# Two transformer blocks in float32 on one core: wait counts in the delta rule, PSUM banks and split order in the feed-forward blocks, and one pool unit's evacuation

## The reference

```python
merged = sigmoid(g_a) * pool_mixer(u_pool, ...) + sigmoid(g_b) * conformer_conv(u_glu, ...)
# delta rule, per head (8 heads) and chunk of 64 tokens (8 chunks)
Lmat = where(strict, (kb @ k.T) * decay, 0)          # Gram matrices
sol = triangular_solve(eye + Lmat, rhs)
v_new = val - kcd @ state
o = qd @ state + a_c @ v_new
state = state * gl + kd.T @ v_new
# feed-forward block (twice), FFN_DIM = 2816
u = causal_dwconv(h @ w_up, conv_w) + conv_b         # 2 x 2816 columns
gate, up = split(u, 2)
h = h + (silu(gate) * up) @ w_down
```

## Time and profile before

| | |
|---|---|
| median of 3 runs | 1963.59 us (1961.83 to 1964.22) |
| profiled execution, its own time | 1957.58 us |
| span of that execution | 1955.6 us |
| mean granted TensorE clock | 0.99 of full speed |

### The profile page before, as it was taken

How to read it: one execution, slowest core, us unless ns; L and a number is a source line. 1 busy time by engine, 2 the same in 40 slices (tenths; PEclk the granted TensorE clock), 3 DMA queues, 4 the chain that set the end, 5 groups by cost and what they waited for, 6 DMA issues and landing times.

```text
span 1955.6 us, 29679 instructions
## 1 busy us (share of the span) xinstructions
PE 1887.9 (97%) x10628; PEld 1525.9 (78%) x10628; DVE 1203.9 (62%) x1851; ACT 787.6 (40%) x1495; POOL 274.3 (14%) x213
## 2 busy tenths in 40 slices
PE   7999999999998899999999999999999999999997
PEld 6888878888887677777778878888776788788886
DVE  5997554333334777677645746747688657467474
ACT  4234343223233555455433423424546534234242
POOL 2532232101022100001011101101100111001012
PEclk9999999999998999999999999999999999999998
DMA  5222323232322111111112332222321122322321
GB/s 193 97 97 97 129 77 102 92 101 93 99 95 76 49 63 58 60 61 49 50 55 90 104 108 86 97 97 97 108 65 44 57 84 99 114 88 91 102 89 72
DMA packets 46945, 170.47 MB, mean 87 GB/s; under 512 B 5344, under 2 KB 5504, under 8 KB 46720
## 3 DMA queue, kind: packets, MB, share of 16 engines
q1 hardware_dynamic: 45648, 165.12, 25.3%
q10 hardware_dynamic: 1200, 3.95, 0.6%
HBM read 166.94 MB, written 2.11 MB: 86 GB/s over the span
## 4 chain that ended last, share of the span: by engine, by line
PE 79%; DVE 10%; ACT 5%; issue 4%; POOL 1%; DVEq 0%; DMA 0%; ACTq 0%; POOLq 0%; SPq 0%
PE ps L256 17%; PE ps L258 17%; PE ps L257 17%; PE ps L268 7%; PE ps L270 6%; PE ps L269 6%; DVE scr L1239 3%; ACT scr L1186 1%; PE ps L644 1%; ACT scr L1411 1%; DVE w_lo L227 1%; ACT Y L1411 1%; PE ps L668 1%; DVE scr L914 1%; DVE scr L1076 1%
## 5 line engine op out<-in xcount | busy, mean ns | idle before, releaser
L227 DVE TENSOR_TENSOR w_lo<-w_raw,w_hi 128x1024 fp32r<-128x1024 f32 x267 | 358.6, 1346 | 190.8 <-ACT w_hi L222 190.4
L222 ACT ACTIVATE w_hi<-w_raw 128x1024 fp32r<-128x1024 f32 x304 | 316.8, 1049 | 267.2 <-PE ps L258 189.4
L256 PE MATMUL ps<-A_hi,w_hi 128*128 128x512 f32 x950 | 370.2, 390 | 1.4 <-DVE scr L1076 1.3
L258 PE MATMUL ps<-A_hi,w_lo 128*128 128x512 f32 x950 | 369.6, 389 | 0.0
L257 PE MATMUL ps<-A_lo,w_hi 128*128 128x512 f32 x950 | 369.6, 389 | 0.0
L256 PE MATMUL ps<-B_hi,w_hi 128*128 128x512 f32 x740 | 288.6, 390 | 3.3 <-issue 2.0
L258 PE MATMUL ps<-B_hi,w_lo 128*128 128x512 f32 x740 | 288.0, 389 | 0.0
L257 PE MATMUL ps<-B_lo,w_hi 128*128 128x512 f32 x740 | 287.9, 389 | 0.0
L256 PEld LDWEIGHTS ps<-A_hi,w_hi 128*128 128x128 f32 x950 | 178.3, 188 | 39.4 <-issue 2.6
L258 PEld LDWEIGHTS ps<-A_hi,w_lo 128*128 128x128 f32 x950 | 178.3, 188 | 37.3
L257 PEld LDWEIGHTS ps<-A_lo,w_hi 128*128 128x128 f32 x950 | 178.3, 188 | 37.2 <-issue 0.2
(11 more groups left out here) (292 smaller groups left out, 2520.0 us busy)
## 6 DMA issues: line engine op xcount, KB each, us to landing
w_raw<-d_ws SPq DMA_DIRECT2D x304, 512.0 KB, 3.5
X<-d_xT SPq DMA_DIRECT2D x4, 512.0 KB, 7.3
X<-d_xT ACTq DMA_DIRECT2D x1, 2048.0 KB, 8.3
d_out<-X SPq DMA_DIRECT2D x4, 512.0 KB, 2.6
scr<-gc_rows ACTq DMA_DIRECT2D x7, 256.0 KB, 3.0
cst<-d_cst SPq DMA_DIRECT2D x1, 800.0 KB, 11.3
par<-d_par SPq DMA_DIRECT2D x1, 344.5 KB, 2.9
scr<-d_pw SPq DMA_DIRECT2D x1, 256.0 KB, 12.2
```

The lines of the kernel that those rows point to most:

```text
L222: nc.scalar.activation(w_hi[:, c], raw[:, c], ACT.Copy).then_inc(S(f"w_hi{s}"), 1)
L227: nc.vector.tensor_tensor(w_lo[:, c], raw[:, c], w_hi[:, c].bitcast(F32), ALU.subtract)\
L256: pe.matmul(ps[bank][:], w_hi[:, c], hi, start=k == 0, stop=False)
L258: last = pe.matmul(ps[bank][:], w_lo[:, c], hi, start=False, stop=k == n - 1)
```

## The change

Five edits. (1) The Gram matmuls signal after chunks 0, 1 and after 2, 3; DVE's masks of the first two chunks wait for the first signal only. (2) Ahead of the output transposes PE runs four filler blocks instead of three, and one fewer after them. (3) In the last head the splits of slots 2 and 3 are queued as in the other heads (ACT's after the first inverse step, DVE's in halves within the inverse's levels), and `B_lo` is made by DVE. (4) In the feed-forward blocks the units use four banks, so that a unit waits for the evacuation of the unit four before; the split that DVE and ACT do in a second-side unit is queued behind that side's chain; down groups begin with three units over n-2 blocks, not two. (5) `gated_pool(2)` stands inside the loop over j.

The final norm's sums go to banks 2 and 3 instead of 4 and 5; `residual_pe` loses options that only the feed-forward blocks used.

```diff
@@ delta_pe: the Gram matmuls of the four chunks signal twice; the filler of the output
             for c in range(NCH):
                 last = pe.matmul(ps[4 - c // 2][:, (c % 2) * 256:(c % 2 + 1) * 256], KQv[:, c, 0, :],
                                  KQ[:, c * 256:(c + 1) * 256], start=True, stop=True)
-            last.then_inc(S("d_gram"), 1)
+                if c % 2:
+                    last.then_inc(S("d_gram"), 1)
...
                 token_major_kq(pe, head_count(h + 1))
-                part(3, 0, 3)
+                part(3, 0, 4)
...
             last.then_inc(S("d_ro"), 1)
             if more:
-                part(3, 3, 5)
+                part(3, 4, 4)
@@ delta_dve
-            dve.wait_ge(S("d_gram"), at("d_gram", 1))
             for c in range(NCH):
+                dve.wait_ge(S("d_gram"), at("d_gram", c // 2 + 1))
                 dve.wait_ge(S("d_dt"), at("d_dt", c + 1))
...
-                if c < 2 and not more:
-                    ahead(dve, split_lo, rnd(U_AOUT, 0), c)
...
+            if not more:
+                dve.wait_ge(S("o_hi"), at("o_hi", 1))
+                v.tensor_tensor(tile(pairB[1], h), O2, tile(pairB[0], h).bitcast(F32), ALU.subtract)\
+                    .then_inc(S("o_lo"), 1)
@@ the feed-forward blocks
+        FBANK = (6, 7, 4, 5)
+        def hidden_segment(pe, r, s, pair, first, end, n, wait=None, fresh=False):
+            if first == 0:
+                pe.wait_ge(S(f"w_hi{s}"), count(f"w_hi{s}", r + 1))
+                pe.wait_ge(S(f"w_lo{s}"), count(f"w_lo{s}", r + 1))
+                if not fresh:
+                    pe.wait_ge(S(f"evac{s}"), count(f"evac{s}", r))
+            last = part_blocks(pe, FBANK[s], s, pair, first, end, n, wait)
+            if end == n:
+                last.then_inc(S(f"unit_done{s}"), 1)
+        def down_pe(pe, base, pair, wait, n, closing):
+            for s in range(3):
+                hidden_segment(pe, rnd(base, 0), s, pair, 0, n - 2, n, wait)
+            for s in range(3):
+                hidden_segment(pe, rnd(base, 0), s, pair, n - 2, n, n, wait)
+            hidden_segment(pe, rnd(base, 0), 3, pair, 0, n, n)
...
@@ ffn_act
-                        if not begin or k == SLOTS - 1:
+                        if not begin and k % 2 == 0:
                             ahead(act, split_hi, r, k + 1)
...
                             .then_inc(S(t + "_c0"), 1)
+                        if side and (not begin or k == SLOTS - 1):
+                            ahead(act, split_hi, r, k + 1)
@@ ffn_dve
-                        if not begin or k == SLOTS - 1:
+                        if not begin and side == 0:
                             ahead(dve, split_lo, r, k + 1)
...
                             v.tensor_tensor(PR[k // 2], FC[0], FC[1], ALU.mult).then_inc(S(t + "_prod"), 1)
+                            if not begin or k == SLOTS - 1:
+                                ahead(dve, split_lo, r, k + 1)
@@ block.vector, branch products
                 if j:
                     ln_lo(j - 1)
+                if j == 1:
+                    gated_pool(2)
             ln_lo(3)
-            gated_pool(2)
             ahead(dve, split_lo, rnd(U_BRANCH, 1), 0)
```

More of the change, by code:

```diff
@@ L1062, in delta_dve, with delta_pool @@
                 evacuate(dve, r, 3, AC[1], 0.5, R[:])
-        def delta_pool(pool, h):
+        def delta_pool(pool, h, more):
             at = head_count(h)
@@ L1077, in evacuate, with residual_pe @@
                                                   op0=op0, op1=op1).then_inc(S(f"evac{k}"), 1)
[L1080 to L1085, removed]
+        def residual_pe(pe, base, pair, wait, late=2):
+            for s in range(2):
+                part_blocks(pe, s, s, pair, KT - late, KT, KT, wait).then_inc(S(f"unit_done{s}"), 1)
             for i in range(2):
-                for s in range(0 if i else 2, SLOTS - (closing and i)):
-                    unit(pe, rnd(base, i), s, pair, n)
+                for s in range(0 if i else 2, SLOTS):
+                    unit(pe, rnd(base, i), s, pair)
         def residual_act(act, base, tag, g, pair, end=False, opened=False, led=False):
@@ L1102, in residual_act, with residual_dve @@
                     square(act, tag, m, tile(X, m))
-        def residual_dve(dve, base, tag, g, pair, bias=None, end=False, opened=False, led=False):
+        def residual_dve(dve, base, tag, g, pair, bias=None, end=False, opened=False, led=False, banks=(0, 1, 0, 1)):
             for i in range(2):
@@ L1110, in residual_dve @@
                     evacuate(dve, r, k, tile(X, m), par_col(bias, m) if bias else 0.0, tile(X, m), ALU.add, ALU.add,
-                             bank=open_bank(k, 4) if opened and i == 0 else k % 2)
+                             bank=open_bank(k, 4) if opened and i == 0 else banks[k])
                     if opened and m < LEAD:
@@ L1138, in hidden_rounds @@
                 one_round(i, False)
+        def hidden_segment(pe, r, s, pair, first, end, n, wait=None, fresh=False):
[13 more added lines that the diff above has]
+            hidden_segment(pe, rnd(base, 0), 3, pair, 0, n, n)
+            for s in range(SLOTS):
+                if closing and s == SLOTS - 1:
+                    hidden_segment(pe, rnd(base, 1), s, pair, 0, n - 1, n)
+                    sums_early(pe, "fin", KT, 2)
+                    hidden_segment(pe, rnd(base, 1), s, pair, n - 1, n, n)
+                else:
+                    hidden_segment(pe, rnd(base, 1), s, pair, 0, n, n)
         def ffn_pe(pe, L, base, inpair, mid, ntag, end=False):
@@ L1155, in wait_mid @@
                     pe.wait_ge(S(t + "_lo"), count(t + "_lo", first + k + 1))
[L1156 to L1162, removed]
+                down_pe(pe, down, mid, wait_mid, n, end and first + n == 22)
         def ffn_act(act, L, base, mid, ntag, next_tag, next_g, next_pair, end=False):
@@ L1253, in ffn_dve @@
                             ahead(dve, split_lo, r, k + 1)
-                            evacuate(dve, r, k, tile(X, 4 * i + k), 0.0, tile(X, 4 * i + k), ALU.add, ALU.add)
+                            evacuate(dve, r, k, tile(X, 4 * i + k), 0.0, tile(X, 4 * i + k), ALU.add, ALU.add,
+                                     bank=FBANK[k])
                 else:
-                    residual_dve(dve, down, next_tag, next_g, next_pair, end=end, led=True)
+                    residual_dve(dve, down, next_tag, next_g, next_pair, end=end, led=True, banks=FBANK)
         def ffn_pool(pool, L, base, mid):
```

37 lines of the change are left out of this document (18 added, 19 removed).

## The result

The changed kernel takes 1945.52 us (4 runs, 1944.75 to 1946.22), against 1962.71 for the kernel before in the same measurement (4 runs, 1957.09 to 1964.22). The ratio is 0.9916, 95% interval 0.9905 to 0.9928: 14 to 19 us faster. The forecast was 1949.6, with 1946 to 1957 as range: right in direction and nearly in size, half a us outside at the fast end.

A forecast was written before the change was run, and what follows sets the result against it. PE was taken as the bound, busy 97% of the span, so only its waits could be won: 1.7 + 6.7 + 2.7 + 4.7 - 1.7 - 0.1 = 14.0 us, and 1963.59 - 14.0 = 1949.6 us, range 1946 to 1957.

The forecast's parts named there:

- Branch products: PE's wait before the unit behind the third pool unit goes, as `gated_pool(2)` runs earlier: saves 1.7 us.
- Delta rule: PE's waits in the heads for DVE's masks, at the output transposes and in the last head go: saves 6.7 us.
- the filler term: Delta heads: one more filler block ahead of the output transposes covers PE's seven waits for ACT: saves 2.3 us.
- state step and `B_lo`: Last delta head: moving the split saves 1.1 us at the state step; `B_lo` on DVE saves 0.7.
- First regular up units: Both feed-forward blocks: with four banks, unit 2 no longer waits for unit 0's evacuation: saves 2 x 1.35 us.
- First down groups: Both feed-forward blocks: a third unit, 4.1 us of matmuls, covers PE's wait for the rounded product: saves 2 x 2.35 us.
- Last down groups: Unit 0's later evacuation delays slot 3's split, so PE waits anew: costs 1.7 us in FFN0, 0.1 in FFN1.
- The chain argument: FFN0's last down group: the rest of the round hangs on DVE's and ACT's chain, so the whole 1.7 us shift stands.
- Edits at nothing: Feed-forward loop rounds: the later split still ends 4.7 to 5.1 us after its evacuation began, inside 5.45; no change in time.
- part of it is taken back: Rival: the split behind the product is late in many loop rounds, so only 5 to 10 us are saved; chance 0.14.
- slower: Rival: the loop's DVE chain in series becomes longer than PE's round of 21.8 us; 1974 us at 23.0; chance 0.04.
- The clock rival: Rival: PE's granted clock falls in part of the feed-forward stages; 2% more time at 1.2 GHz cancels the gain; chance 0.02.

The follow-up runs named there:

- e7: The changed kernel with all feed-forward splits queued ahead of the chain again, four banks and three units kept: 1943.33 us, ratio 0.9908.
- e12: The changed kernel with up units back in two banks and each down group's first two units waiting separately: 1946.74 us, ratio 0.9933.
- e6: The changed kernel with two instead of three units ahead of the late blocks in every down group: 1941.40 us, ratio 0.9898.
- e4: The changed kernel with the last down group's splits queued one unit earlier on ACT and DVE: 1945.55 us, ratio 0.9931.
- e5: e4, with the attention's opening no longer waiting for the evacuation of FFN0's units 6 and 7: 1940.55 us, ratio 0.9893.
- e10: e5 with the splits of the feed-forward loop back ahead of the chain, four banks and three units kept: 1939.13 us, ratio 0.9886.
- e1: The kernel before with only `gated_pool(2)` moved inside the loop over j: 1958.10 us, ratio 0.9995.
- e2: The kernel before with only the Gram signals, the filler blocks and the last head's changes: 1955.10 us, ratio 0.9978.
- e11: The changed kernel with two units ahead of the late blocks and splits ahead of the chain, four banks kept: 1953.97 us, ratio 0.9960.

## Why the prediction came out as it did

- **Branch products**: forecast 1.7, measured 1.79.
- **Delta rule**: masks and filler 4.9, measured 5.43 without a wait left. Each head gets back 0.38 us at L590 and 0.38 at L774, so the filler term (0.33 a head) was the small one; state step and `B_lo` 1.8, measured 1.79.
- **First regular up units**: 2 x 1.35, measured 1.40 and 1.43. Size and reason were right: the four banks alone bring 1.54 (e7). What the prediction didn't see is that the new order alone would have brought 0.77 (e12), and that on top of the banks it costs 0.1.
- **First down groups**: 2 x 2.35, measured 2.47 twice. The mechanism as the prediction put it ("That covers 2.35") is one of two, each enough by itself. Without the order of the splits the wait to cover would have been 3.9 us, not 2.35, since PE arrives 1.54 sooner. The step took the wait of before as fixed while another edit moved its start; that three units cover it anyway, by 0.2 us in e7, is luck. And with the new order the third unit, which the prediction credited with the whole term, brings nothing: e6 does without it and has the same -2.47.
- **Last down groups**: +1.7 and +0.1, measured +1.82 and +0.41. The chain argument was right in its core, as e4 shows (evacuations 4.3 us apart whatever PE does). The term is the price of the third unit: in e6, without it, the places stand at -0.42 and -0.36. What I missed was the end of it, the opening's wait of 0.69 us, which is needless since the change (e5).
- **Edits at nothing**: the steady loop lost nothing, and the rivals "part of it is taken back" and "slower" did not come. But the two readings behind it were off, as one second side of the changed kernel shows:

```profile
1115.69 0.69 DVE L1077 SCALAR_TENSOR_TENSOR scr<-ps,R 128x512 f32<-128x512 f32 x1 [1.54 <-PE ps L270]
...
1119.32 0.69 DVE L1269 TENSOR_TENSOR scr<-scr 128x512 f32<-128x512 f32 x1
1119.93 1.22 DVE L227 TENSOR_TENSOR w_lo<-w_raw,w_hi 128x1024 fp32r<-128x1024 f32 x1
1121.75 1.62 DVE L227 TENSOR_TENSOR w_lo<-w_raw,w_hi 128x1024 fp32r<-128x1024 f32 x1 [0.61 <-ACT w_hi L222]
```

  The chain without the split takes 4.3 us, not 3.5 (its first tap now waits for ACT), and with it 5.5, a little more than PE's 5.45. What hides it is the first side's slack, 1.54 us of idle DVE in the row above, not room within the second side. And the split behind the product is not the slow one: it takes 1.22 us, because POOL starts its `B_lo` only when that split is nearly over. The slow one is the split after it (1.62 here, 1.63 in the first sides of the loop, 1.59 in the earlier trace rows before the change), which starts while POOL is at work.
  The order isn't free, though: e7 and e10 show 0.1 us at each first up unit and 0.4 at each last group against it.
- **The sum**: -14.0 forecast, -14.55 at the touched places. The carry from profile to median was the mis-sized step: "the median of the runs is 6.0 above that execution, and I carry that over". These 6.0 us are no property of the kernel: they are how three executions fell. In the experiments' groups the kernel before ran 54 more times, with a median of 1959.6, and the time goes with the mean granted clock of the run: 1957.0 to 1960.4 us at 0.990 (30 runs), 1959.8 to 1962.6 at 0.989 (10), 1962.0 to 1964.1 at 0.988 (10), 1964.3 to 1964.7 at 0.987 (4). Part of that is, as far as e1 and e2 show it, clock tails behind waits that the change removes; the changed kernel's median is 0.5 above its profile. That is why the time came out 4.1 us under the forecast, while the profiled one came out 1.4 over it (1944.98 against 1943.6).

The clock rival asked whether four banks would slow PE. Two rounds of up units in the changed kernel, to set beside the earlier trace rows:

```profile
1070.00:1113.60 43.60, 43.60 (x194) 36.12 (x193) 36.37 (x45) 20.73 (x26) 6.65 (x5) 1.00 0.34 109
```

The granted clock is 1.00 with PE busy throughout. The Trainium skill ("TensorE: Matmul & The Clock Gate", § A second HAM failure mode: psum-queue depth-cycling) tells of banks cycled with brief idling between groups; here the groups follow without idling, and no oscillation is seen. The clock did matter, from the other side: in e1, e2, e4 and e11 it fell behind waits of PE of 2.2 to 3.8 us.

## What to carry to other kernels

Before you price the removal of a wait, ask whether its end moves with its start: where a slower engine's chain sets the end, time won ahead of it is handed back there, and a wait upstream and one downstream are one wait. When units get banks of their own, look for every wait elsewhere that was written for the shared banks. And a stop of PE can cost a slow stretch behind it in some executions (here 1.6 us behind a stop of 2.2), so a profile without that stretch understates what the stop is worth in the median. Read the granted clock of all runs, not of the profiled one alone, before you carry a distance between profile and median over to a forecast.

## What the runs showed of the hardware

PE's clock fell to the lower level behind some waits and not behind others of the same length. Behind the wait of 2.2 us at the first down groups it did not fall in the profile of before (two cases), and fell in three of four cases of e1 and e2, at a cost of 1.6 us each time. Behind waits of 3.5 to 3.8 us (e4's opening, e11's late blocks) it fell in all three cases.

Two places with the same work in all kernels scatter in the same way. Behind the attention's wait of 3.7 us every other kernel took 0.4 to 1.0 us longer than the profiled execution of before, e1 and e2 too, which change nothing near it (e5 and e10 have a wait of their own there), and the final norm's eight sums took 1.05 or 1.86 us. The rows of before and of the changed kernel:

```profile
1943.67 1.05 PE L440 MATMUL ps<-ones,SQ 128*128 128x1 f32 x8 [1.44 <-ACT SQ L411]
```

```profile
1930.21 1.86 PE L440 MATMUL ps<-ones,SQ 128*128 128x1 f32 x8 [1.44 <-ACT SQ L411]
```

Same operations behind the same idle time of 1.44 us, at a granted clock of 0.77 and of 0.50 in the window of 4.5 us around them. That makes 1.8 us which the changed kernel's profile lost against before's without any cause in its code.

The scatter of the kernel before, 7 us, goes with the clock, and has its size: between 0.990 and 0.987 of full speed lie 0.003 x 1957 = 5.9 us of lost time, and the means of its runs at these two values are 6.2 us apart (1958.3 and 1964.5). What stays open is where the longer ones lose it. Two tails of 1.6 us are half; the rest of the profiles' scatter lies behind other waits (1.5 us between 255 and 290 us, 1.0 at the attention, 0.8 at the norm). Only one execution of each kernel is profiled, so which of them the longer ones had was not seen.

DVE's split of 128x1024 was slow only where POOL was at work first. In the changed kernel the one that started at 1100.00, while POOL's `B_lo` ran from 1099.20 to 1100.55, took 1.63 us; the one from 1109.14, during which POOL started at 1110.17, took 1.22. Over its whole trace 109 splits start while POOL is busy, with a median of 1.48 us, and 51 have POOL start during them: none of those takes over 1.23.
